# Chunked linear-attention and RWKV-7 mixer layer: the inverse's block products, its operands and strict masks take another place in a round of the second stage

## The reference, cut to what matters

```python
def rwkv7_recurrence(r, w, k, v, kk, a, s0):
    def step(s, inp):
        r_t, w_t, k_t, v_t, kk_t, a_t = inp
        sa = jnp.einsum('bhij,bhj->bhi', s, -kk_t)
        s = (s * w_t[:, :, None, :] + sa[..., None] * (kk_t * a_t)[:, :, None, :]
             + v_t[..., None] * k_t[:, :, None, :])
        y = jnp.einsum('bhij,bhj->bhi', s, r_t)
        return s, y
...
x = x + rms_norm(einsum(concat([o_gla, (y + bonus) * silu(z_r)]), w_out), norm_post)
```

## Time and profile before

| | |
|---|---|
| median of the runs | 2321.36 us (2316.69 to 2324.19) |
| the profiled execution's own time | 2315.25 us, its span 2313.5 us |
| TensorE busy | 2242.2 us, 97% of the span |
| VectorE busy | 1448.1 us, 63% |
| ScalarE busy | 1284.4 us, 56% |
| GpSimd busy | 578.2 us, 25% |
| mean DMA rate | 106 GB/s |

### The profile page before, as it was taken

One profiled execution on the slowest core, in us unless ns is written; L12 is line 12 of the kernel. 1 busy time (PEld: TensorE's weight loads), 2 busy tenths in 40 slices (PEclk: granted clock), 3 DMA queues, 4 the chain that ended last, 5 costly groups with the idle time before them and its releaser, 6 DMA issues. The chain is left out here.

```text
span 2313.5 us, 72365 instructions
## 1 busy us (share of the span) xinstructions
PE 2242.2 (97%) x31109; PEld 1704.8 (74%) x31109; DVE 1448.1 (63%) x2699; ACT 1284.4 (56%) x2757; POOL 578.2 (25%) x1070
## 2 busy tenths in 40 slices
PE   7999999999999998889999999999999998899998
PEld 5777777777777776777888888888888886544443
DVE  6444545444455554567777777777777777456675
ACT  8355555555555544645666666666666664343333
POOL 0000000000000000355555555555566565000000
PEclk9999999999999999999999999999999999999999
DMA  6212222222333331222222333232223234666675
GB/s 245 69 56 70 80 79 89 79 79 90 105 108 117 101 101 50 52 59 70 72 72 78 83 87 87 78 81 67 72 82 87 84 88 141 204 213 214 223 237 182
DMA packets 217278, 244.62 MB, mean 106 GB/s; under 512 B 110080, under 2 KB 159552, under 8 KB 212608
## 3 DMA queue, kind: packets, MB, share of 16 engines
q1 hardware_dynamic: 211056, 217.44, 30.8%
q10 hardware_dynamic: 5904, 22.55, 2.7%
HBM read 141.83 MB, written 98.10 MB: 104 GB/s over the span
## 5 line engine op out<-in xcount | busy, mean ns | idle before, releaser
L2111 PE MATMUL first<-h,w_hi 128*128 128x256 f16 (+1 forms) x2496 | 419.1, 272 | 0.0
L2070 POOL TENSOR_TENSOR r_inv_tmp<-r_inv 64x30 f32<-64x30 f32 (+14 forms) x480 | 265.8, 554 | 412.8 <-DMA r_inv<-scratch_blocks 376.5
L748 PE MATMUL d<-h,w_hi 128*128 128x256 f16 (+1 forms) x2176 | 351.6, 270 | 0.0
L2111 PE MATMUL first<-h,w_lo 128*128 128x256 f16 (+1 forms) x1248 | 337.8, 272 | 0.0
L748 PE MATMUL d<-h,w_lo 128*128 128x256 f16 (+1 forms) x1088 | 290.6, 270 | 0.0
L2072 POOL TENSOR_TENSOR r_inv<-r_inv,r_inv_tmp 64x30 f32<-64x30 f32 (+14 forms) x480 | 279.7, 583 | 37.6
L2111 PEld LDWEIGHTS first<-h,w_hi 128*128 128x128 f16 x2496 | 237.6, 98 | 50.4 <-issue 18.9
L748 PEld LDWEIGHTS d<-h,w_hi 128*128 128x128 f16 x2176 | 209.5, 98 | 33.6 <-issue 3.9
L2013 POOL MEMSET r_run_s<- 128x128 f16 x1 | 0.2, 204 | 917.9 <-POOLq L390 917.9
L748 PE MATMUL first<-h,w_hi 128*128 128x256 f16 (+1 forms) x1168 | 184.5, 268 | 5.0 <-DVE w_lo L1236 3.1
L2111 PE MATMUL r_d<-h,w_hi 128*128 128x256 f16 (+1 forms) x960 | 158.8, 271 | 0.8 <-DVE carry_s L2742 0.8
(11 more groups left out here) (393 smaller groups left out, 5129.2 us busy)
## 6 DMA issues: line engine op xcount, KB each, us to landing
h<-in_x SPq DMA_DIRECT2D x33, 512.0 KB, 3.7
r_ops<-in_x SPq DMA_DIRECT2D x33, 512.0 KB, 4.2
out_y<-r_ops SPq DMA_DIRECT2D x33, 512.0 KB, 7.4
scratch_hT<-h SPq DMA_DIRECT2D x16, 1024.0 KB, 7.0
h<-scratch_hT ACTq DMA_DIRECT2D x15, 1024.0 KB, 7.1
scratch_mg<-m_hl SPq DMA_DIRECT2D x33, 256.0 KB, 2.0
r_zr<-scratch_zr SPq DMA_DIRECT2D x33, 256.0 KB, 3.5
r_bon<-scratch_bonus SPq DMA_DIRECT2D x33, 256.0 KB, 5.1
```

What stands on the lines that cost most here:

```text
L748: mm = pe.matmul(out, lhs(k, a, w), rhs(k, a, w), start=(n == 0), stop=(n == len(terms) - 1))
L2070: step(pool.tensor_tensor(tmp, inv[0:n, 0:u, u:u + 1].to_broadcast([n, u, w]), inv[0:n, u:u + 1, u + 1:32].to_broadcast([n, u, w]), ALU.mult))
L2111: mm = pe.matmul(out, lhs(k, a, w), rhs(k, a, w), start=(m == 0), stop=(m == 3 * KT - 1))
```

## The change

Three tables are rewritten in the round's second half, and the numbering of finished banks is adapted to it.

- TensorE: `xs` moves from behind `turn:4` to behind `scores:4`. Of x8's six pieces four stand ahead of `meet:3` (before: two), and two behind `xs`.
- ScalarE: `high:0` moves behind both `rnorm`.
- VectorE: `clamp:1` moves ahead of `even:2`; `k_prime` ahead of `next:2`; `low:0` from behind `clamp:1` to behind `join_o:3`; `beta` and `a` ahead of `td`; both `strict` ahead of the x8 mix.
- Banks go round as before (`ROUND_NO`), but since `xs` now finishes ahead of x8, the count in `d_full` is taken from a second numbering, `FULL_NO`, by the last piece. All waits on `d_full` use it.

```diff
@@ PE_BODY
-    x8*2 meet:3 scores:4 out x8*4 inner:4 unknowns:3 turn:4 xs variance:1 out x10*2 advance:3 solve:4 join:4
+    x8*4 meet:3 scores:4 xs out x8*2 inner:4 unknowns:3 turn:4 variance:1 out x10*2 advance:3 solve:4 join:4
@@ ACT_BODY
-    join_e:2 affine:0 squares:2 out gamma taken:x0 odd:2 turned:3 high:0 rnorm:0 out rnorm:1 z1:3 join_e:3
+    join_e:2 affine:0 squares:2 out gamma taken:x0 odd:2 turned:3 rnorm:0 out rnorm:1 high:0 z1:3 join_e:3
@@ DVE_BODY
-    clamp:0 even:2 mixed:x0 keep_w:3 clamp:1 low:0 out unit:0 unit:1 next:2 join_o:3 k_prime mixed:x2 out
-    -td masked:4 zc:3 beta a mixed:x8 strict:0 out strict:1 even:3 keep_w:4 normed:1 rkk next:3 join_o:4 gated:1
+    clamp:0 clamp:1 even:2 mixed:x0 keep_w:3 out unit:0 unit:1 k_prime next:2 join_o:3 low:0 mixed:x2 beta out a
+    -td masked:4 zc:3 strict:0 out strict:1 mixed:x8 even:3 keep_w:4 normed:1 rkk next:3 join_o:4 gated:1
@@ after ROUND_KEYS
+def full_order():
+    ends = {}
+    for n, (job, arg) in enumerate(j for jobs in PE_JOBS for j in jobs):
+        if job == "piece":
+            ends[arg[:2]] = n
...
+    return sorted(ROUND_KEYS, key=ends.get)
+FULL_NO = {key: n for n, key in enumerate(full_order())}
@@ claim
-                return bank_of(key), m
+                return bank_of(key), FULL_NO[key]
```

More of the change, by code:

```diff
@@ L1552 @@
 ROUND_KEYS = list(ROUND_NO)
+def full_order():
[3 more added lines that the diff above has]
+            ends[arg[:2]] = n
+        elif job == "out":
+            ends["out", arg[0], arg[1] // 6] = n
+        elif job in ("xs", "kn", "bs"):
+            ends.update({(arg, job + str(k)): n for k in range(2)})
+        elif job == "rank":
+            ends.update({(arg[0], r % arg[1]): n for r in ("lw%d", "la%d")})
+        elif job == "centre":
+            ends.update({(job, arg, k): n for k in range(2)})
+        elif job == "variance":
+            ends[job, arg] = n
+    return sorted(ROUND_KEYS, key=ends.get)
+FULL_NO = {key: n for n, key in enumerate(full_order())}
 AT = {}
@@ L1558 @@
 EARLY = ("x12", "x4", "x6")
-assert [ROUND_NO[0, r] for r in EARLY] == [0, 1, 2]
+assert [ROUND_NO[0, r] for r in EARLY] == [FULL_NO[0, r] for r in EARLY] == [0, 1, 2]
 def rwkv_phase(nc, t, c):
@@ L1893, in get_ow @@
                 if j == 0:
-                    m = ROUND_NO[LAST - 1, "x10"]
+                    m = FULL_NO[LAST - 1, "x10"]
                     sp.wait_ge(d_full.sem, d_full.at(m, 1))
@@ L1901, in get_npost @@
             def get_npost():
-                m = ROUND_NO[LAST, "x10"]
+                m = FULL_NO[LAST, "x10"]
                 sp.wait_ge(d_full.sem, d_full.at(m, 1))
@@ L1911, in fetch @@
                 if tile >= 2:
-                    sp.wait_ge(d_full.sem, d_full.at(ROUND_NO["out", tile - 2, 1], 1))
+                    sp.wait_ge(d_full.sem, d_full.at(FULL_NO["out", tile - 2, 1], 1))
                 sp.dma_start(m_c[:, slot, 0], t["mg"][b][:, i]).then_inc(*mc_in[slot].up(n))
@@ L1923, in get_tw @@
                 if i == 0:
-                    sp.wait_ge(d_full.sem, d_full.at(ROUND_NO[LAST, "x10"], 1))
+                    sp.wait_ge(d_full.sem, d_full.at(FULL_NO[LAST, "x10"], 1))
                     sp.wait_ge(ow_ok.sem, 2 * KT)
@@ L2119, in piece @@
                 n = tiles(b) * P
-                out, m = bank_of((b, r)), ROUND_NO[b, r]
+                out, m = bank_of((b, r)), FULL_NO[b, r]
                 if h == 0 and third == 0:
@@ L2361, in project_out @@
                 h, sixth = n // 6, n % 6
-                m = ROUND_NO["out", tile, h]
+                m = FULL_NO["out", tile, h]
                 out = bank_of(("out", tile, h))
@@ L2585, in centred @@
             def centred(tile):
-                act.wait_ge(d_full.sem, d_full.at(ROUND_NO["centre", tile, 1], 1))
+                act.wait_ge(d_full.sem, d_full.at(FULL_NO["centre", tile, 1], 1))
                 for k in range(2):
@@ L2666, in out_squares @@
                 tile, h = arg
-                act.wait_ge(d_full.sem, d_full.at(ROUND_NO["out", tile, h], 1))
+                act.wait_ge(d_full.sem, d_full.at(FULL_NO["out", tile, h], 1))
                 if tile:
```

18 lines of the change are left out of this document (9 added, 9 removed).

## The result

| | before | after |
|---|---|---|
| median of 4 runs | 2321.62 us | 2384.24 us (2377.38 to 2386.27) |
| span of the profiled execution | 2313.5 us | 2375.6 us |
| ratio | | 1.0272 (95% interval 1.0253 to 1.029) |

The account below looks back on a forecast made before the run. TensorE, 99% busy, was taken to bound the second stage. Fourteen rounds at 2.5 us (35.0), plus 2.4, 0.3, 2 and 1, less 2.3, made 38.4 us slower: 2360 us, 8-in-10 range 2336 to 2378.

Parts of the forecast that it names:

- the distance: In each round, from the inverse's store to the turn (td), by way of DRAM and four loads: taken as 6.5 us.

Follow-up runs that it names:

- e2: The changed kernel with low:0 (VectorE) and high:0 (ScalarE) back where they stood before the change: 2339.5 us, ratio 1.0084.
- e1: The changed kernel with the inverse's store and loads ahead of put_m:0 in SyncE's queue instead of behind it: 2348.13 us, ratio 1.0127.
- e3: The kernel before with only low:0 late (behind k_prime) and high:0 behind both norms: 2418.63 us, ratio 1.0426.
- e4: The changed kernel with TensorE's order of the kernel before, the other engines as changed: 2418.98 us, ratio 1.0428.
- f2: The changed kernel with TensorE's order, low:0, high:0 and the x8 mix back as before; only clamp:1, k_prime, beta and a stay early: 2322.10 us, ratio 1.0007.

## What to carry over

Before an operation is moved, list everything that waits for it on each engine: the queue behind the waiting instruction, and the writers of every tile that it reads. One 0.7 us subtraction held up a DMA queue (36 us) and, through its input tile, another engine (e2 is 8.6 us below e1). Where a wait recurs in every round, each tenth of a us in its price counts 14 times. Read all rows of the trace before and not two, and keep room above them: the distance had a mean of 6.55 there, of 6.45 and 6.55 in e3 and e4, and of 6.98 in the changed kernel. Add what the granted clock can lose behind the wait. And tables that are written for each other can't be judged one at a time: the change without its part on TensorE was 35 us worse than all of it.

## What the hardware showed that I had not expected

- A wait of 3.3 us on TensorE was followed by 6 us at a granted clock of 0.50 (e3). In the changed kernel waits of 2.8, 2.3 and 3.3 us were followed by a lower clock (rounds 3, 6 and 8), and one of 3.1 (round 9) by none.
- The bonus sums stall 0.5 to 2.2 us once in three rounds, in nearly the same places in e1, e2, e3, e4, f2 and the changed kernel, with nothing that the profile shows to wait for; in the kernel before once. A packet of the instruction queue lies in the same 4 us as one of them (1529 to 1533 of the changed kernel), but one also lies beside the bonus sums in a round of before that doesn't stall (1560 to 1563). The cause stays open; nothing was tried on it.
- The last of the inverse's four loads took 1.0 to 1.8 us longer to land in five of 13 rounds of the changed kernel, and in none of e3 and e4, whose store is as late. Why stays open.
